# Attention on one core: row sums by GpSimd additions, a running maximum held in PSUM, and a division moved to the output projection

## The reference

```python
def block_attention(q, k, v):          # 8 heads, q 2048 x 96, k 2304 x 96, v 2304 x 64
    ...
    s = jnp.einsum('bqhd,bkhd->bhqk', qblk, k).astype(jnp.float32) * scale
    p = jax.nn.softmax(s, axis=-1).astype(v.dtype)
    return jnp.einsum('bhqk,bkhd->bqhd', p, v)
...
y_lat = jnp.concatenate([o_att.reshape(B, S, MLA_HEADS * MLA_V), retention_out(y_r, rg, g_ret)], axis=-1) @ w_o
```

## Time and profile before

| | value |
|---|---|
| median of 3 runs | 2978.84 us |
| span of the profiled execution, first to last instruction | 2978.0 us |
| PE busy in the span | 2749.8 us (92%) |
| DVE busy | 2099.8 us (71%) |
| ACT busy | 1441.5 us (48%) |
| POOL busy | 348.9 us (12%) |
| attention stage, from first score tile to last store issued | 868 to 1767 us |
| `mix_out` stage | 1767 to 2000 us |

### The profile page before, as it was taken

The page is one execution under the profiler, slowest core; times in us unless marked ns, Lnnn a source line. Parts: engine busy times, 40 slices in busy tenths (PEclk is TensorE's granted clock), DMA queues, the critical chain, the costliest instruction groups (busy, mean ns, idle before and its releaser), DMA issues. The chain is left out here.

```text
span 2978.0 us, 57085 instructions
## 1 busy us (share of the span) xinstructions
PE 2749.8 (92%) x20805; PEld 2244.1 (75%) x20805; DVE 2099.8 (71%) x3131; ACT 1441.5 (48%) x2146; POOL 348.9 (12%) x377
## 2 busy tenths in 40 slices
PE   5999999899959999999999979992999999999996
PEld 2877777688847766766766748882989988988995
DVE  3555554677749999999999965547667667657666
ACT  3555555322237767767766742112444444444444
POOL 0111111222210000000000002210101101101102
PEclk8999999999979999999999989995999999999998
DMA  7544443422230110110110024334667767767778
GB/s 244 176 158 151 149 149 113 134 76 76 62 61 3 37 33 10 37 32 11 37 34 10 5 85 153 134 116 132 206 191 226 225 190 207 226 179 219 226 217 306
DMA packets 267042, 375.33 MB, mean 126 GB/s; under 512 B 35571, under 2 KB 186646, under 8 KB 265174
## 3 DMA queue, kind: packets, MB, share of 16 engines
q1 hardware_dynamic: 257334, 337.83, 35.5%
q0 software_dynamic: 9504, 34.61, 5.0%
HBM read 286.61 MB, written 85.77 MB: 125 GB/s over the span
## 5 line engine op out<-in xcount | busy, mean ns | idle before, releaser
L2012 PE MATMUL ebank<-gathered_T,w_gate_up 128*128 128x256 f32 x4608 | 552.5, 282 | 20.8 <-issue 13.8
L2012 PEld LDWEIGHTS ebank<-gathered_T,w_gate_up 128*128 128x128 f32 x4608 | 548.3, 190 | 24.3 <-issue 23.4
L1285 PE MATMUL abank<-head_qT,head_kT 96*128 96x512 f32 x1728 | 413.9, 400 | 22.8 <-DVE head_qT L1394 17.0
L1285 PEld LDWEIGHTS abank<-head_qT,head_kT 96*128 96x128 f32 x1728 | 325.6, 191 | 104.2 <-issue 29.3
L1365 ACT ACTIVATE scores<-scores 128x1536 f32<-128x1536 f32 x192 | 274.3, 1476 | 232.9 <-DVE scores L1424 232.9
L1424 DVE TENSOR_TENSOR scores<-scores,abank 128x1536 f32<-128x1536 f32 x192 | 322.6, 1747 | 47.9 <-PE abank L1305 44.8
L1360 ACT ACTIVATE scores<-abank 128x512 f32<-128x512 f32 x576 | 325.4, 601 | 41.7 <-PE abank L1285 16.0
L501 PE MATMUL bank<-w_in_sb,h_T 128*128 128x512 f32 (+1 forms) x1296 | 292.5, 384 | 9.1 <-DVE h_T L702 9.1
L1315 PE MATMUL abank<-scores,head_v 128*64 128x256 f32 x2304 | 291.0, 388 | 1.2 <-ACT scores L1365 1.2
L2026 PE MATMUL ebank<-w_down,hidden_T 128*128 128x512 f32 x1152 | 281.1, 399 | 3.5 <-DVE w_down L2244 3.4
L501 PEld LDWEIGHTS bank<-w_in_sb,h_T 128*128 128x128 f32 x1296 | 243.7, 190 | 44.0 <-DVE h_T L702 7.2
(11 more groups left out here) (285 smaller groups left out, 3637.0 us busy)
## 6 DMA issues: line engine op xcount, KB each, us to landing
w_gate_up_whole<-in_w_exp_gate SPq DMA_DIRECT2D x48, 1024.0 KB, 5.4
w_gate_up_whole<-in_w_exp_up SPq DMA_DIRECT2D x48, 1024.0 KB, 9.0
w_down_whole<-in_w_exp_down SPq DMA_DIRECT2D x192, 256.0 KB, 5.8
ada_rest<-in_w_ada SPq DMA_DIRECT2D x16, 1024.0 KB
x_tile<-in_x_all SPq DMA_DIRECT2D x18, 512.0 KB
scratch_h<-h_T_whole SPq DMA_DIRECT2D x18, 512.0 KB, 2.7
ada_w<-in_w_ada SPq DMA_DIRECT2D x4, 2048.0 KB
chunk_h_T_whole<-scratch_h SPq DMA_DIRECT2D x16, 512.0 KB
```

The costliest lines, as they stand in the source:

```text
L1285: m = pe.matmul(banks[S_BANKS[kt % 4]][:, :], kT[u][:, kp, k], qT[u][:, qp, q], start=(n == 0), stop=(n == 2))
L2012: x = pe.matmul(banks[f % 3][:, j * CAP:(j + 1) * CAP], w_gu[c][:, wp, j, k, o:o + P], xsT[:, xp, k, :], start=(k == 0 and n == 0), stop=( ...
```

## The change

- **Row sums.** The ones beside the values are gone (`v1` is 64 wide) and PE's 12 small matmuls in each of six groups too. GpSimd adds the six probability groups of a block into `acc[j % 2]`, 128 x 1536, by five additions (two inputs in SBUF). PE then sums the three parts of `acc` over the partitions with 12 matmuls (`prob_sum`), for b - 1, after the tenth score tile of b + 1.
- **Maximum.** Instead of groups of three tiles DVE takes pairs (`PAIRS` = 9): eight operations of 128 x 1024. The first has both inputs in SBUF, the others read one input from and (but for the last) write to a tile of two PSUM banks, `mx_psum`. There is one fold instead of two.
- **Output.** ACT copies the undivided output (`raw_output`, 128 x 256), DVE takes the reciprocal after it (`inverse`), and both are stored, in three DMAs instead of one; the eight multiplications are gone.
- **Buffers.** A score copy of b + 1 waits for GpSimd's addition of b - 1; PE waits for `raw` and `inverse` of b - 2.
- **Loop.** The first pair of heads is written out as well.
- **`mix_out`.** Two more DMAs for each tile bring the inverses, each row repeated on 64 partitions; DVE multiplies (`scale_att`, 128 x 512) before ACT rounds.

```diff
-                    dve.tensor_tensor(mx[:, :, :], s[:, 0:G, :], s[:, G:2 * G, :], ALU.max).then_inc(sg["max_keys"].sem, 1)
+                    sg["shifted"].wait(dve, b - 1)
+                    dve.tensor_tensor(dst[:, :, :], s[:, 0:2, :], s[:, 2:4, :], ALU.max).then_inc(sg["max_keys"].sem, 1)
                 else:
-                    sg["max_keys"].wait(dve, b, g - 1)
-                    dve.tensor_tensor(mx[:, :, :], mx[:, :, :], s[:, g * G:(g + 1) * G, :], ALU.max).then_inc(sg["max_keys"].sem, 1)
+                    sg["max_keys"].wait(dve, b, n - 1)
+                    dve.tensor_tensor(dst[:, :, :], s[:, 2 * n:2 * n + 2, :], mx_psum[:, :, :], ALU.max).then_inc(sg["max_keys"].sem, 1)
...
         @block.gpsimd
         def _(pool):
-            for u in range(2):
-                pool.memset(v1[u][:, :, DV:], 1.0).then_inc(ones_set, 1)
+            def turn(pair, j, b, more):
+
+                p, a = sc[j % 2], acc[j % 2]
+                sg["probs"].wait(pool, b, 2)
+                sg["out_psum"].wait(pool, b - 2)
+                pool.tensor_tensor(a[:, :, :], p[:, 0:G, :], p[:, G:2 * G, :], ALU.add).then_inc(sg["summed"].sem, 1)
+                for g in range(2, GROUPS):
+                    sg["probs"].wait(pool, b, g + 1)
+                    sg["summed"].wait(pool, b, g - 1)
+                    pool.tensor_tensor(a[:, :, :], a[:, :, :], p[:, g * G:(g + 1) * G, :], ALU.add).then_inc(sg["summed"].sem, 1)
...
-                for kt in range(g * G, (g + 1) * G):
+            def prob_sum(j, b):
+
+                ps, a = banks[5 + j % 2], acc[j % 2]
+                sg["summed"].wait(pe, b)
+                for t in range(G):
                     for c in range(4):
-                        m = pe.matmul(ps[32 * c:32 * c + 32, HB:HB + P], v1[u][:, kt, DV:DV + 32], p[:, kt, c * P:(c + 1) * P],
-                                      start=False, stop=(kt == T - 1), skip_group_check=True)
-                return m
+                        m = pe.matmul(ps[32 * c:32 * c + 32, HB:HB + P], ones[:, :], a[:, t, c * P:(c + 1) * P],
+                                      start=False, stop=(t == G - 1), skip_group_check=True)
+                m.then_inc(sg["out_psum"].sem, 1)
...
             def fold(b):
 
-                for g in (1, 2):
-                    sg["max_keys"].wait(dve, b, GROUPS - 2 + g)
-                    dve.tensor_tensor(mx[:, 0, :], mx[:, 0, :], mx[:, g, :], ALU.max).then_inc(sg["max_keys"].sem, 1)
+                sg["max_keys"].wait(dve, b, PAIRS - 1)
+                dve.tensor_tensor(mx[:, 0, :], mx[:, 0, :], mx[:, 1, :], ALU.max).then_inc(sg["max_keys"].sem, 1)
...
+            def scale_att(m, u):
+
+                att_loaded.wait(dve, m, u)
+                settled(dve)
+                x = mt_whole[u][:, 1, 0:KH, :]
+                dve.tensor_tensor(x, x, inv[u][:, :, :], ALU.mult).then_inc(sg["att_scaled"].sem, 1)
```

More of the change, by code:

```diff
@@ L1209, in loop @@
         def loop(eng, turn):
-            with eng.Fori(0, H // 2 - 1) as pair:
+            for j in range(2 * NB):
+                turn(0, j, j, True)
+            with eng.Fori(1, H // 2 - 1) as pair:
                 for j in range(2 * NB):
@@ L1258, in turn @@
             def turn(pair, j, b, more):
-                if j % NB == NB - 2 and not isinstance(pair, int):
+                if has_before(pair, j):
+                    store(pair * 2 + ((j - 1) // NB), (j - 1) % NB, b - 1)
+                if j % NB == NB - 2 and not final_pair(pair):
                     sg["s_psum"].wait(sp, b + 1)
@@ L1262, in turn @@
                     load_kq(pair * 2 + (2 + j // NB), j // NB)
[L1263 to L1266, removed]
+                if j % NB == NB - 1 and not final_pair(pair):
+                    sg["valued"].wait(sp, b)
+                    settled(sp)
                     load_v(pair * 2 + (2 + j // NB), j // NB)
             loop(sp, turn)
+            store(H - 1, NB - 1, BLOCKS - 1)
             sg["out_stored"].wait(sp, BLOCKS - 1)
@@ L1336, in turn @@
                         max_spread(b + 1)
-                m.then_inc(sg["out_psum"].sem, 1)
+                    if not more and g == 3:
+                        prob_sum((j - 1) % 2, b - 1)
+                m.then_inc(sg["valued"].sem, 1)
             sg["rounded"].wait(pe, 0)
@@ L1442, in turn @@
                 if more:
-                    for g in range(1, GROUPS):
-                        maximum((j + 1) % 2, b + 1, g)
+                    for n in range(1, PAIRS):
+                        maximum((j + 1) % 2, b + 1, n)
                     fold(b + 1)
-                if j:
-                    output(j - 1, b - 1)
+                if has_before(pair, j):
+                    inverse((j - 1) % 2, b - 1)
                 if more:
@@ L1452, in turn @@
                         shift((j + 1) % 2, b + 1, g)
-                if j == 2 * NB - 1:
-                    output(j, b)
+                else:
+                    inverse(j % 2, b)
             for n in range(3):
                 split(0, 0, n)
-            for g in range(1, GROUPS):
-                maximum(0, 0, g)
+            for n in range(1, PAIRS):
+                maximum(0, 0, n)
             fold(0)
@@ L1697, in turn @@
                     probabilities(m - 2)
+                if ahead:
+                    scale_att(m + 2, u)
+            for u in range(2):
+                scale_att(u, u)
             for n in range(4):
```

107 lines of the change are left out of this document (71 added, 36 removed).

## The result

The changed kernel takes 3167.97 us (median of four runs: three took 3166.94 to 3168.21 us; the fourth, a slow one of 4036.45 us at a granted clock of 0.63 where the others have 0.93, counts in no ratio), the kernel before 2980.68 us in the same comparison. The ratio is 1.0616, with a 95% interval of 1.0591 to 1.0642: slower, and the two medians lie 187 us apart. Forecast were 3143 us, and 3015 to 3215 as the range. The profiled execution took 3166.94 us and has a span of 3165.2 us.

What follows compares the result with a forecast made beforehand. PE was taken to bound the kernel, DVE only just behind. Attention +157, last turn with store +5 and `mix_out` start +2 sum to +164 on the 2978.84 us median: 3143 us, range 3015 to 3215.

Steps and rivals of the forecast that it cites:

- The hold: In the attention, a DVE instruction with two SBUF inputs waits for GpSimd's running instruction, then takes its own time less 0.14 us.
- GpSimd's addition: In the attention, one GpSimd addition of 1536 columns takes 3.46 us; five make 17.3 us per turn and fit.
- Maxima through PSUM: In the attention, a DVE maximum 1024 wide takes 1.25 us, eight 10.0 us, with no added wait for the PSUM chain.
- The turns: Attention turns, from one run of six shifts to the next: 14 of 34.2 us, 7 of 32.8, 6 of 29.8, 4 of 28.5.
- +157: Added time over the attention's 31 turns: 1001 us where 31 x 27.22 = 844 stood.
- the step that ACT is usually ready before DVE's first maximum: In the attention, ACT's exponential of group 1 ends first, so GpSimd's first addition holds the first maximum, ending at 14.35, not 11.3.
- PE's slower clock: Rival in the attention: PE, idle some 6 us before the first transpose, slows; up to 3.8 us in 10 turns, +38; chance 0.13.
- the race that I had counted as a favour: In the attention, DVE might take its first maximum before GpSimd's first addition, margin at most 0.38 us; part of the kindly case.
- Tail and start: The last attention turn to its store costs +5 us; four more DMAs queued before `w_o` in `mix_out` cost +2 us.
- The cover of 2.9 us: In `mix_out`'s loop, a tile's rest is ready 2.9 us early, hiding multiplication and loads: nothing, up to 28 us if loads land late.
- That DVE isn't held: Rival in the attention: the hold is shared or released within an instruction, turn 25.05 us, total 2918 us; chance 0.12.
- The mild case, where the hold falls kindly: Rival in the attention: first maximum precedes the addition, copy not held, 3030 us; other variants 3107, 3070, 2962; chance 0.30.

## Why the prediction was right

- **The hold, step by step.** That a DVE instruction with two SBUF inputs waits for GpSimd's running addition, and that two in a row let an addition pass between them, was read from 128 x 512 instructions of the retention stage and holds for 1536 columns. In the turn shown the first maximum ends 1.10 us behind the addition, which is its own 1.23 less 0.13, where 0.14 was put. Without additions the turn falls to 25.8; the forecast for a DVE that isn't held was 25.05.
- **GpSimd's addition.** Put at 3.46 us; 3.42 at the least, 3.51 in the median. The estimate from the Trainium skill (GPSIMD Engine Reference, 3.1), 3.4, was as good. That it would change the sum by under 5 us was too low by the prediction's own rate (0.37 us an addition for 46 us): 0.06 us less make some 7.
- **Maxima through PSUM.** Put at 1.25, measured 1.229, and the chain through PSUM adds next to no wait: six in a row take 7.54 us, 1.26 each.
- **The turns.** Forecast 34.2 (rests and rounding), 32.8 (rests alone), 29.8 (no rests) and 28.5 (the last pair); the trace has means of 35.0, 33.8, 29.7 and 30.1. All together 1025.3 us against 1001: the sum was 24 us short, 11 in the first kind, 7 in the second, 6 in the last.
- **What was luck in it.** The old turns were put at 27.22 each, 844 us, and took 855.9 with the loop's edges; this hides 12 of the 24 us, so that +157 stands against +169. The turns without rests agree only as a mean: they took 33 us twice, 28.5 to 29.7 three times and 25.6 once. And the step that ACT is usually ready before DVE's first maximum failed in 16 of 31 turns, since PE's slower clock, listed only as a rival, also delays the scores that ACT copies. Half of the first maxima were thus not held, and wherever rests followed, both met an addition: the race that I had counted as a favour brought the other hold instead.
- **PE's clock.** Listed as a rival with up to +38 us. It came about in part: the groups behind the fold took 4.77 us instead of 2.9 in the turn above. The last pair's last three turns, where these groups are on the path, are 2.2 us over the forecast each.
- **Tail and start.** +5 was 5.7, +2 was 3.2. The output projection's loop, for which nothing was put, with up to 28 us in the range, cost 7.6. The cover of 2.9 us was read from a tile further on; the third tile, where PE waits now, had 0.25 in the kernel before (rest ready at 1807.98, wanted at 1808.23).
- **The rivals of the other side.** That DVE isn't held is refuted: its price was 2918, and what measures near it, 2932.77 us, is the kernel without additions. The mild case, where the hold falls kindly, didn't come as a whole: half of the first maxima were taken in time, but GpSimd does go before the second rest, and the copy is held in every turn (1.0 to 2.1 us).

## What to carry to other kernels

Before moving work to GpSimd, list what the busy DVE reads. In this kernel every DVE instruction with two SBUF inputs waited for the end of a running GpSimd instruction that reads SBUF, and the fast copy also for one that only writes; the price is set by the length of GpSimd's instruction and not by DVE's own. Two such DVE instructions in a row cost two GpSimd instructions when more of these are queued. It isn't enough to move the large ones to PSUM operands; here five small ones, 4.3 us of work in a turn, gave back more than PE had gained. Once they had one SBUF input each or lay on GpSimd itself the kernel was still 1% slower than before (3010.69 us); it became 1% faster (2944.73) only when PE's second transpose went one group earlier too. What that earlier transpose would do to the kernel before, without the change, was not tried; PE was the bound there.

## What was not expected of the hardware

- GpSimd's writing alone holds the fast copy for longer than the 1 to 2 us expected (2.29 us on average instead of 0.43) and leaves instructions with two SBUF inputs untouched (0.692 and 0.948).
- PE's clock falls inside a turn: after 6 us of idle time the next 5.8 us were granted 0.55, and it was back at 1.00 in the stretch after. A wait of DVE thus costs PE more than the wait, and by way of the scores it even sets which DVE instruction is held next.
- Whether GpSimd's first addition starts 0.2 to 0.6 us before DVE's first maximum or 0.9 us or more behind it changes which instructions are held, but doesn't shorten the turns with rests: where ACT rounds they take 33.3 to 35.9 us with the maximum held and 34.0 to 36.0 without, where it doesn't 32.8 with and 32.4 to 35.7 without. Without rests it shows: 33 us with the maximum held against 25.6 to 29.7 without where ACT rounds, and 30.7 against 28.5 in the last pair.
